# Sample compression in two 64-row groups, and raw cache tiles asked for as their slots fall free

## The reference

```python
def compress(raw, p, c):
    B, NC = raw.shape[:2]
    z = raw + p['cmp_pos'][c][:, None, :]
    z = jnp.swapaxes(z, 2, 3).reshape(B, NC, NSA_KV_HEADS, CMP_BLK * HEAD_DIM)
    return jax.nn.gelu(z @ p['phi_w1'][c] + p['phi_b1'][c]) @ p['phi_w2'][c]
```

## Time and profile before

| | |
|---|---|
| median of 3 runs | 1674.8 us (1664.6 to 1676.3) |
| the profiled execution | 1676.7 us, span 1674.6 us |
| TensorE busy, weight loads busy | 1298 us (78%), 946 us (56%) |
| VectorE, ScalarE, GpSimd busy | 668 us, 464 us, 241 us |
| sample stage | from about 589 us to 1050 us |
| TensorE's mean granted clock | 0.851 of full |
| DMA busy from 167 to 209 us, from 460 to 586 us | 0.2, 0.0 (page, line DMA) |
| granted clock, slice from 419 to 461 us | 0.5 (page, line PEclk) |

### The profile page before, as it was taken

The page is one execution under the profiler, slowest core; times in us unless marked ns, Lnnn a source line. Parts: engine busy times, 40 slices in busy tenths (PEclk is TensorE's granted clock), DMA queues, the critical chain, the costliest instruction groups (busy, mean ns, idle before and its releaser), DMA issues. The chain is left out here.

```text
span 1674.6 us, 22414 instructions
## 1 busy us (share of the span) xinstructions
PE 1298.0 (78%) x7251; PEld 945.6 (56%) x7251; DVE 667.8 (40%) x1931; ACT 464.1 (28%) x1094; POOL 241.3 (14%) x365
## 2 busy tenths in 40 slices
PE   6799961476689937877787885797898549999991
PEld 4799960233556625665565663496787324554540
DVE  4733346333266612444443352536404711211215
ACT  2000023310035523556554452110511201111112
POOL 1000003000100042442424400000000031111112
PEclk9999985566579957989999996699978869999996
DMA  6244248200200086465756633320325246566424
GB/s 162 51 88 88 54 169 351 52 0 15 78 1 1 1 217 163 127 182 170 200 161 174 171 100 114 65 78 23 124 78 209 88 171 234 221 243 227 179 94 166
DMA packets 173342, 213.09 MB, mean 127 GB/s; under 512 B 78136, under 2 KB 142632, under 8 KB 166408
## 3 DMA queue, kind: packets, MB, share of 16 engines
q1 hardware_dynamic: 148424, 150.05, 29.5%
q0 software_dynamic: 24832, 61.94, 11.9%
HBM read 214.98 MB, written 39.37 MB: 152 GB/s over the span
## 5 line engine op out<-in xcount | busy, mean ns | idle before, releaser
L2708 PE MATMUL bank<-wgu,memtok 128*128 128x512 f32 x384 | 170.8, 598 | 1.8 <-DVE memtok L2911 1.8
L1877 ACT ACTIVATE ZTs<-bank 64x256 f32<-64x256 f32 x320 | 121.0, 378 | 67.6 <-PE bank L1710 64.1
L1656 DVE COPY ZTs<-bank 64x256 f32<-64x256 f32 x192 | 81.0, 422 | 116.0 <-PE bank L1710 114.1
L2708 PEld LDWEIGHTS bank<-wgu,memtok 128*128 128x128 f32 x384 | 73.6, 192 | 94.4 <-issue 94.4
L1718 PE MATMUL bank<-ZTs,w1s 128*128 128x256 f32 x512 | 116.9, 388 | 3.4 <-ACT ZTs L1877 3.4
L1718 PEld LDWEIGHTS bank<-ZTs,w1s 128*128 128x128 f32 x512 | 98.4, 195 | 26.5 <-ACT ZTs L1877 13.3
L1605 POOL DMA_DIRECT2D rawc<-in_cache_nsa_kv x128 | 75.3, 590 | 180.6 <-PE bank L1779 155.2
L260 PE MATMUL bank<-h_high,w_low 128*128 128x272 f32 x384 | 81.4, 293 | 9.0 <-DVE h_low L370 5.0
L1763 PE MATMUL bank<-cst,kv 128*128 128x128 f32 x256 | 51.5, 336 | 47.2 <-DMA kv<-in_cache_nsa_kv 41.6
L2730 PE MATMUL bank<-wdn,yT 128*128 128x512 f32 x192 | 86.5, 593 | 1.5 <-DVE yT L2916 0.9
L260 PE MATMUL bank<-h_high,w_high 128*128 128x272 f32 x384 | 80.4, 291 | 0.0
(11 more groups left out here) (573 smaller groups left out, 2459.6 us busy)
## 6 DMA issues: line engine op xcount, KB each, us to landing
kv<-in_cache_nsa_kv SPq DMA_DIRECT2D x256, 128.0 KB, 2.9
wgu<-in_exp_w_gate SPq DMA_DIRECT2D x24, 1024.0 KB, 5.0
wgu<-in_exp_w_up SPq DMA_DIRECT2D x24, 1024.0 KB, 7.3
wdn<-in_exp_w_down SPq DMA_DIRECT2D x24, 1024.0 KB, 5.1
rawc<-in_cache_nsa_kv POOLq DMA_DIRECT2D x128, 128.0 KB, 4.3
ring<-in_cache_nsa_kv POOLq DMA_DIRECT2D x112, 128.0 KB, 2.8
rows_dram<-ring POOLq DMA_DIRECT2D x24, 512.0 KB, 13.3
ring<-in_w_in SPq DMA_DIRECT2D x44, 256.0 KB, 3.7
```

The source lines that it names most:

```text
L1656: ins = copy(ZT[HD * a:HD * a + HD, :, :, g, 8 * j:8 * j + 8], z_bank(j)[HD * g:HD * g + HD, 256 * a:256 * a + 256].rearrange("p (v n c) - ...
L1877: return act.activation(dst, src, ACT.Copy)
L2708: mm = pe.matmul(gemm_big[n % 2][:, :].rearrange("p (m f) -> p m f", m=2), XT[:, n % 2, k, :], w[:, :, k, :], start=(k == 0), stop=(k == K ...
```

## The change

The rows of `phi_w1` are laid out anew: the 64 numbers of head 0 lie in partitions 0 to 63 and those of head 1 in 64 to 127, with the weights twice, once for each half. `copy_z` becomes one copy of a whole bank, and tiles alternate between ScalarE and VectorE. `hide` contracts 64 rows for one head and 64 for the other, 128 columns each, into two banks; its 64 steps a sequence are cut up and put behind `keys(b, 3)` to `keys(b, 7)`, with 6 before and 6 behind the transposes of the weights. The 12 raw tiles are turned before `keys(b, 1)` and `keys(b, 2)`, and `keys(b, 1)` moves behind `window_scores(b)`. The weights need twice the room: those for the keys go to `xT`, the residual stream, which is written to DRAM in the first stage and read back at the end of the sample stage. They are loaded during prompt attention, and those for the values right behind the first raw tiles. GpSimd no longer waits for `scores(b, 0)`, and reads its page numbers ahead of the waits. Not shown are the same moves on ScalarE and VectorE (their loops also run from n = 1).

```diff
+        x_flat = xT[:, :, :].rearrange("p k n -> p (k n)")
+        x_dram = nc.dram_tensor("x_dram", (P, KT * NT), F32).ap()
...
+                    sp.wait_ge(turned_out, 10)
+                    sp.dma_start(x_dram, x_flat).then_inc(x_saved, 16)
                     w = I["xa_wkv"][0].rearrange("(k p) n -> p k n", p=P)
                     for n in range(8):
...
+                    sp.wait_ge(x_saved, 16)
...
+            load_phi2(sp, w2, sem_)
+        def load_phi_rows(sp, dst, kv, sem_):
+            for g in range(G):
+                sp.dma_start(dst[HD * g:HD * g + HD, :, :], I["phi_w1"][0, kv].rearrange("(t d) h -> d t h", d=HD))\
+                    .then_inc(sem_, 16)
+        w1k_here = sem("w1k_here")
+        def load_phi2(sp, w2, sem_):
...
+                @block.sync
+                def _(sp):
+                    load_phi_rows(sp, x_flat[:, 0:32 * P].rearrange("p (t h) -> p t h", h=P), 0, w1k_here)
...
-            w1 = [t7(f"w1s{kv}", [P, 16, P]) for kv in range(2)]
+            w1 = (x_flat[:, 0:32 * P].rearrange("p (t h) -> p t h", h=P), t7("w1v", [P, 32, P]))
...
-            ZT = t7("ZTs", [P, 2, 16, G, NCB])
+            ZT = t7("ZTs", [P, 4, 16, NCB])
...
-            COPIER = [0, 1, 0, 0, 1, 0, 0, 1, 0, 1, 0, 0, 1, 0, 1, 0]
+            COPIER = [0, 1] * (CT // 2)
...
-                return range(AHEAD + 12 * (n - 2) // 7, AHEAD + 12 * (n - 1) // 7)
+                return (range(0), range(4, 8), range(8, 16))[n] if n <= 2 else ()
+            HIDDEN = {3: (0, 10), 4: (10, 20), 5: (20, 32), 6: (32, 42), 7: (42, 52)}
+            TAIL = 58
+            def pieces(u0, u1):
+                return [(kv_, range(max(u0, 32 * kv_) - 32 * kv_, min(u1, 32 * kv_ + 32) - 32 * kv_))
+                        for kv_ in range(2) if max(u0, 32 * kv_) < min(u1, 32 * kv_ + 32)]
+            h_bank = (work[2], work[1])
...
                     eng.wait_ge(z_mm, b * CT + (j + 1))
-                    for g in range(G):
-                        for a in range(2):
-                            ins = copy(ZT[HD * a:HD * a + HD, :, :, g, 8 * j:8 * j + 8],
-                                       z_bank(j)[HD * g:HD * g + HD, 256 * a:256 * a + 256].rearrange(
-                                           "p (v n c) -> p v c n", v=2, c=16))
-                    ins.then_inc(z_out[who], 1)
+                    copy(ZT[:, :, :, 8 * j:8 * j + 8],
+                         z_bank(j)[:, :].rearrange("p (u n c) -> p u c n", u=4, c=16)).then_inc(z_out[who], 1)
...
-                    sp.dma_start(past[:, :], K["past"]).then_inc(c7_const, 16)
-                    sp.wait_ge(s_w2z, 1)
-                    load_phi(sp, w1, w2, s_w2)
...
                     def load_kv(b):
...
                     load_raw(sp, SP, lambda j: raw0_here[j - CT // 2], 0, late, None)
+                    load_phi_rows(sp, w1[1], 1, s_w1v)
+                    sp.wait_ge(s_w2z, 1)
+                    load_phi2(sp, w2, s_w2)
+                    sp.dma_start(past[:, :], K["past"]).then_inc(c7_const, 16)
...
                         load_kv(b)
+                    sp.wait_ge(h_mm, NB)
+                    sp.dma_start(x_flat, x_dram).then_inc(x_back, 16)
+                    sp.wait_ge(x_back, 16)
...
                     with pool.Fori(0, NB - 2) as b:
-                        load_raw(pool, POOL, lambda j: rawc_here[j], b + 2, early, b * CT + CT, b * 3 + 2)
-                        load_raw(pool, POOL, lambda j: rawc_here[j], b + 2, late, b * CT + CT)
+                        page = [page_numbers(POOL, b + 2, CT // 2 * i) for i in range(2)]
+                        load_raw(pool, POOL, lambda j: rawc_here[j], b + 2, early, b * CT + CT, None, page[0])
+                        load_raw(pool, POOL, lambda j: rawc_here[j], b + 2, late, b * CT + CT, None, page[1])
...
-                    pe.wait_ge(s_w2, 80)
                     def turn_raw(b, tiles):
...
                         for j in tiles:
...
                             for i in range(4):
-                                mm = pe.transpose(z_bank(j)[:, P * i:P * i + P], raw_slot(j)[:, i // 2, i % 2, :], ident)
+                                mm = pe.transpose(z_bank(j)[:, P * i:P * i + P], raw_slot(j)[:, i % 2, i // 2, :], ident)
                             mm.then_inc(z_mm, 1)
...
-                    def hide(b, kv_):
-                        if kv_ == 0:
+                    def hide(b, kv_, us=range(32)):
+                        if kv_ == 0 and us[0] == 0:
...
                                 pe.wait_ge(z_out[who], b * COPIER.count(who) + COPIER.count(who))
-                        for c in range(16):
-                            mm = pe.matmul(work[2][:, 256 * kv_:256 * kv_ + 256], w1[kv_][:, c, :],
-                                           ZT[:, kv_, c, :, :].rearrange("p g n -> p (g n)"),
-                                           start=(c == 0), stop=(c == 15))
-                        if kv_ == 1:
+                        for u in us:
+                            a, c = u // 16, u % 16
+                            for g in range(G):
+                                rows = slice(HD * g, HD * g + HD)
+                                mm = pe.matmul(h_bank[g][:, P * kv_:P * kv_ + P], w1[kv_][rows, 2 * c + a, :],
+                                               ZT[rows, 2 * kv_ + a, c, :], start=(u == 0), stop=(u == 31))
+                        if kv_ == 1 and us[-1] == 31:
                             mm.then_inc(h_mm, 1)
...
                     def compressed_keys(b):
...
                     def turn(b, h):
-                        bank_ = (work[1], gemm_big[0])[h]
+                        bank_ = (gemm_small[0], gemm_big[0])[h]
                         for i in range(4):
...
                     turn_raw(0, range(CT))
+                    pe.wait_ge(w1k_here, 32)
                     hide(0, 0)
+                    pe.wait_ge(s_w1v, 32)
                     hide(0, 1)
+                    pe.wait_ge(s_w2, 48)
                     turn_raw(1, range(AHEAD))
                     compressed_keys(0)
...
-                    keys(0, 1)
...
                     for b in range(NB):
...
                         window_scores(b)
-                        for n in range(2, NKT):
-                            keys(b, n)
+                        def hide_part(u0, u1):
+                            for kv_, us in pieces(u0, u1):
+                                hide(b + 1, kv_, us)
+                        for n in range(1, NKT):
                             if more:
                                 turn_raw(b + 1, with_step(n))
-                            if n == 3 and b:
+                            keys(b, n)
+                            if n == 2 and b:
...
                             if n == 5:
                                 scores(b, 0)
+                            if more and n in HIDDEN:
+                                hide_part(*HIDDEN[n])
                         scores(b, 1)
                         if more:
-                            hide(b + 1, 0)
+                            hide_part(52, TAIL)
                         turn_new(b)
                         turn(b, 0)
                         turn(b, 1)
                         if more:
-                            hide(b + 1, 1)
+                            hide_part(TAIL, 64)
                         values_new(b)
...
                         if more:
...
                         turn_raw(b + 2, ahead[2:4])
                         if more:
                             keys(b + 1, 0)
-                            keys(b + 1, 1)
...
                     def compressed(b):
...
-                            ins = act.activation(hid[:, kv_, :, :].rearrange("p g n -> p (g n)"),
-                                                 work[2][:, 256 * kv_:256 * kv_ + 256], ACT.Gelu_apprx_tanh,
-                                                 bias=hb[:, kv_:kv_ + 1])
+                            for g in range(G):
+                                ins = act.activation(hid[:, kv_, g, :], h_bank[g][:, P * kv_:P * kv_ + P],
+                                                     ACT.Gelu_apprx_tanh, bias=hb[:, kv_:kv_ + 1])
```

More of the change, by code:

```diff
@@ L408, in build @@
             hT, hmT, vecs = pT[:, 0:KT, :], pT[:, KT:2 * KT, 0:NM], pT[0:V_END, 2 * KT, 0:P]
-            vecs_here, rest_here = sem("vecs_here"), sem("rest_here")
+            vecs_here, rest_here, x_saved = sem("vecs_here"), sem("rest_here"), sem("x_saved")
             x_here = [sem(f"x_here{j}") for j in range(2)]
@@ L1564, in build @@
             rawc2 = ring[:, :, :, :].rearrange("p u k n -> p (u k n)").rearrange("p (j a c n) -> p j a c n", a=2, c=2, n=P)
-            c7_const, s_w2z, s_w2 = sem("past_here"), sem("w2s_zero"), sem("phis_here")
+            c7_const, s_w2z, s_w2 = sem("past_here"), sem("w2s_zero"), sem("w2s_here")
+            s_w1v, x_back = sem("w1v_here"), sem("x_back")
             rawc_here = [sem(f"rawc_here{j}") for j in range(CT)]
@@ L1610, in raw_slot, with load_raw @@
```

(22 more changed lines are left out.)

## The result

The changed kernel takes **1695.5 us** (median of 4 runs, 1690.8 to 1699.3), the kernel before 1674.0 beside it: ratio 1.013, 95% interval 1.009 to 1.018. The forecast was 1637, its range ended at 1671. The profiled execution took 1699.3 us, its span is 1697.3.

The account below looks back on a forecast made before the run. No engine was full; a chain of waits, 30 us of kv fetching and 20 behind it, set the cycle. From 1676.7: -17 (head) - 1.5 (first cycle) - 5 x 4.3 + 1 = 1637.7, written as 1637 us; range 1612 to 1671.

Parts of the forecast that it names:

- first cycle: Sample stage, first cycle between window_scores: 47.7 us before, kv tiles already there, 1.5 us less.
- middle cycles: Sample stage, five cycles of 50.7 us: each falls by 4.3 to 46.4 us, including 1.3 of waiting.
- seventh cycle: Sample stage, cycle without raw tiles: 44.3 us before, rebuilt sum the same within 0.5, so no gain.
- the rest of the kernel: Outside the sample stage: writing xT to DRAM may delay the next weights, +1 us, ends 0 and 4.
- The fetches: Sample-stage cycles: kv and raw tile requests now collide, adding 1.3 us of waiting to each of five cycles, ends 0 and 8.
- the end at 28: Both streams, 8.8 MB at 236 GB/s, end 28 us after window_scores; TensorE wants the last kv tile at 26.0.
- the first rival: Sample-stage cycles: kv tiles starve at a third of 236 GB/s, cycle some 52.5 us, kernel 1668 us; chance 0.12.
- The head: Start of the sample stage: earlier raw requests bring window_scores(0) to about 651, 17 us less, ends 10 and 22.
- weights late: Low end for the stage's head: value weights arrive late and the gain is 10 us instead of 17.
- The rebuilt cycle: One sample-stage cycle summed from window_scores on, at full clock, before kv waiting is added: 45.1 us.
- The hidden product: Every hide: 128 products of 128 columns a sequence, 14.1 us if array halves work together, 28.2 if in turn.
- the second (halves in turn): Rival at every hide: array halves work in turn, 14.1 us more in each of 8 sequences, kernel 1743 us; chance 0.13.

Follow-up runs that it names:

- The last experiment: Changed kernel with GpSimd's wait for scores(b, 0) back, value weights awaited before raw tiles of sequence 1, page numbers read before that wait: 1636.9 us, 0.978 of before.

## Why the prediction was wrong

Its sum was 1637.7, and the profiled execution of the change took 1699.3. By its own steps, with starts from the windows of the change:

| step | forecast | measured | missed |
|---|---|---|---|
| `window_scores(0)` | 651 | 665.6 | 14.6 |
| first cycle | 46.2 | 45.3 | -0.9 |
| middle cycles | 5 x 46.4 | 5 x 55.7 | 46.3 |
| seventh cycle | 44.3 | 43.2 | -1.1 |
| the rest of the kernel | +1 | | 2.7, the remainder |

**The fetches: the step that failed.** The term "1.3 us of waiting on each of the five cycles, with ends 0 and 8" stands for all that the collision adds, and that is the 10.4 us between 45.3 and 55.7. The waiting itself measured 7.5 us a cycle, just inside the far end; the 3.1 us of slower work behind the waits have no term in the sum at all. Two errors are in the waiting. First, I let both streams end together at the full rate, "the end at 28", and compared only the last kv tile with its turn. But `keys` take the tiles one by one, each with a piece of product behind it, and the middle ones were the late ones: `keys(b, 5)` at +24.7. Pieces moved ahead won 4 of the 10 us back, though they left the streams as they were. Second, I took raw tiles to come "one by one and not all at once" and used that against the first rival. They came with all 32 requests inside the kv fetch. Its premise, a third of the rate or 79 GB/s for kv, was close while TensorE stood: in the cycle before the one shown, from 717 to 738 us, the queues were

```profile
q0 software_dynamic: 1154, 3.15, 66.2%
q1 hardware_dynamic: 1926, 1.75, 40.9%
```

1.75 MB in 21 us, 83 GB/s. The first rival's cycle of 52.5 us holds 7.4 us of waiting for the 7.5 measured, and is short of 55.7 only by what the slower work costs; its chance of 0.12 was too low, since the earlier trace rows had shown nearly this share.

The Trainium skill (DMA: Bandwidth & Descriptors, section Queues, rings and completion order) says that a DMA engine takes turns between its queue rows packet by packet. By that a queue with larger packets would get more bytes. In the rows above q0 moves 2.7 KB a packet and q1 0.9, and q0 gets 1.8 times the bytes, which agrees in direction; its packets are only 0.6 of q1's, so a strict one for one isn't what these rows count. No run changed the size of the pieces, so what sets the share is not shown.

**The head: mis-sized by 15 us** (14.6). Raw tiles of sequence 0 were in and turned when I said. What failed is "2 MB behind the raw tiles at half the rate, 118 GB/s, 17 us, so about 630": they landed at 644. SyncE asked for them only at 605.5, and the raw tiles of sequence 1 were in the queues from 608. My end for "weights late", 10 us of gain, was too kind too: it was 3. The last experiment shows that the order of requests was the fault, since with the raw tiles of sequence 1 held back the weights are used from 627.4, and `window_scores(0)` comes at 645.6, ahead of my 651.

**What held.** The rebuilt cycle: 45.1 without a collision, 45.3 measured with the wait back, as the mean of the middle cycles. The hidden product: 2 x 7.42 = 14.8 us for 14.1; in pieces of 10 steps 2.50 us, where the forecast had 2.19 and 0.28 for the change of form. Copies of 0.59 and 0.69 us for 0.60 and 0.69. The round trip of xT: nothing. Of the rivals, the second (halves in turn) was a real mechanism with a price of 91 us where I had 106, but this order avoids it.

So the forecast's 1637 us is met to the microsecond, but by a kernel with two gates the change lacked: with the raw requests held back in the loop (45 us) and in the head (14 us). That it comes out to the microsecond is luck: this kernel's first `window_scores` is 5 us earlier than forecast, its first cycle 1.4 us longer and its middle cycles 0.6 shorter.

## What to carry to other kernels

A prefetch asked for as early as its slot allows can take bandwidth from the fetch that the engine waits for, as it did here; where the two streams fill the DMA engines, hold back the one that isn't urgent, and read what it needs (its page numbers) before the gate and not behind it. To price such a meeting, set every tile's landing against its own turn and against what is queued behind that turn, not the last tile against the last turn; and a wait in a trace that seems to cost only an idle engine, as GpSimd's 21 us did, may be what keeps two streams apart.

## What the runs showed that I had not expected

- The waits cost clock as well. With the wait the middle cycles ran at a granted clock of 1.00 and 39.3 us of TensorE work, without it at 0.91 to 0.94 and 42.3 us on average for the same instructions: 3 of the 10 us.
- The same missing wait cost 7, 30 or 45 us, by the loop around it, and 1.9, 3.2 or 10.4 us of a middle cycle.
- A DMA request can grow dear on the issuing side: 32 kv requests took SyncE 24 us before and 31 beside the 32 raw requests of the change, and the two of 1 MB took 15 us in the change and 9 where GpSimd held back. Full DMA engines alone don't explain it: with 16 and 20 raw requests beside them the 32 kv requests took 24 us, with the engines as full. The cause is not shown.
